# Gate and up projection of 20 feed-forward tiles by a seven-product 2x2 block scheme

## The chip, the cores and the metric

The kernel runs on one core of one Trainium2 chip. The metric is device microseconds of one execution, as the median of three runs. The engines are TensorE (PE, with its weight loads shown as PEld), VectorE (DVE), ScalarE (ACT), GpSimd (POOL) and SyncE (SP, which here issues the loads of the weights).

## The reference, cut to what matters

One decoder layer for 512 prompt tokens and 64 sample tokens, 576 in all, model width 1024. After three attention branches and an output projection comes the feed-forward part, in fp32. Its width is 2816, which is 22 tiles of 128:

```python
h = layer_norm(ALPHA * x + mix @ w_o, ln1_w, ln1_b)
ff_gate, ff_up = split(h @ w_ffn_in, 2)            # (576 x 1024) @ (1024 x 5632)
y = layer_norm(ALPHA * h + (silu(ff_gate) * ff_up) @ w_ffn_out, ln2_w, ln2_b)
```

## The kernel before

Everything is held transposed: features on the partitions, tokens along the free axis, in two halves of 288 tokens (`TH`). To keep fp32 accuracy each operand is split in two fp32r parts, a high part (the value rounded) and a low part (the rest). A 128 x 128 weight tile then takes three matmuls of 288 columns: high weights by low x, low weights by high x, high by high (lines 706 to 708).

A weight unit is 8 such tiles, 1024 x 128 values, 512 KB. SP loads it into one of four raw buffers `w_raw` (line 1057), as soon as the unit that was four before it has been used. ACT copies it into one of three buffers `w_hi` (line 1249). DVE writes the low part `w_lo` over the raw buffer (line 623; for some early units POOL does that).

A feed-forward tile `j` has a gate unit (`fg`) and an up unit (`fu`), each with two halves of tokens. Each of these four outputs is summed in one of three PSUM banks over 8 x 3 = 24 matmuls, so a tile has 96. For `fg`, ACT copies the bank (line 1279) and takes a tanh, and DVE makes the silu times two from both (line 1545). For `fu`, DVE multiplies by the bank (line 1568) and at once splits the result into `hidden_hi` and `hidden_lo` (lines 1571, 1572). These two hold all 22 tiles, since the output projection (`y`, lines 736 to 738) reads all of them.

One list, made by `schedule()`, sets the order of all work. Each engine walks it and issues its own part in that order, with semaphores between the engines. `ffn_order(j)` says in which order the four outputs of a tile come; the end of LayerNorm 1 (`center`, `norm`; `x_hi` on ACT, `x_lo` on DVE line 1590) is laced into tiles 0 and 1. Behind the loop over the tiles come the output projection and LayerNorm 2.

POOL adds the eight tiles of a LayerNorm mean in three steps (line 1204), issues some loads, and makes decay terms of one attention branch earlier (line 1145). It has nothing to do in the feed-forward loop.

Of the kernel before, what the change touches and what calls it, by code (L numbers as in the profile page):

```python
# [96 lines left out]
def ffn_order(j):  # L97

    if j == 0:
        return [("fg", 0, 0), ("fu", 0, 0), ("fg", 1, 0), ("fg", 0, 1), ("fu", 0, 1), ("fg", 1, 1)]  # L100
# [4 lines left out]

def weight_units():
# [47 lines left out]
    for j in range(FT_):  # L154
# [21 lines left out]
def schedule():  # L176
# [194 lines left out]
def build_decoder_layer(nc, a, outs_):  # L371
    ctx = ExitStack()
    with ctx:
# [189 lines left out]
        def moving(key, k):  # L563
# [55 lines left out]
        def split_lo(eng, u):  # L619
# [47 lines left out]
        def _(pe):  # L667
# [11 lines left out]
            def main(key):  # L679
# [5 lines left out]
                bank = take(main_bank(key))  # L685
# [1248 lines left out]
```

## Time and profile before

| what | value |
|---|---|
| median of three runs (lowest to highest) | 1152.78 us (1147.83 to 1152.86) |
| span of the profiled execution | 1145.7 us (no other time of it is given) |
| PE busy | 1090.5 us, 95%, 8128 matmuls |
| DVE, ACT, POOL busy | 641.9, 399.0, 210.3 us |
| matmuls of the gate/up and input projections | lines 706 to 708, 1504 each at x |
| moved by DMA | 105.82 MB |

Busy time is the sum of an engine's instructions. Matmuls overlap in PE's pipeline, so the pace of matmuls is read from the distance of two equal places in the loop, not from the duration of one. The feed-forward tiles run from about 693 us to about 978 us of the span.

### The profile page before, as it was taken

Reading aid. Unit: us, or ns where it says so; the run is one execution under the profiler, and the core shown is the slowest. Engines: PE = TensorE matmul, PEld = TensorE weight load, DVE = VectorE, ACT = ScalarE, POOL = GpSimd, SP = SyncE. Lnnn points to the kernel's source line nnn. Section 1 sums busy time; section 2 is a strip of 40 time slices with the busy share of each in tenths; the row PEclk is TensorE's granted clock in tenths of the full one; section 3 lists DMA queues with packets and bytes.
Section 4 is the critical chain, followed back from the end, with each engine's and each line's share of the span. In section 5 each row is a group of like instructions: output and inputs, shape, how many; then the busy total and the mean of one; then the engine's idle time right before and its main releaser. Section 6 shows DMA issues by size and latency. Waiting matters only on the chain.

```text
span 1145.7 us, 19556 instructions
## 1 busy us (share of the span) xinstructions
PE 1090.5 (95%) x8128; PEld 1051.9 (92%) x8128; DVE 641.9 (56%) x1022; ACT 399.0 (35%) x769; POOL 210.3 (18%) x266
## 2 busy tenths in 40 slices
PE   6799999998989998899999998999999999999996
PEld 5799888987989998889999987999999999999985
DVE  4833276345669989864654787444444444322455
ACT  3634255542345454315222255212221222111245
POOL 3521000012176563551000140000000000011130
PEclk9899899999999999999999999999999999999998
DMA  8456111135321111243232440332323232223422
GB/s 270 93 145 210 38 56 53 41 111 169 90 74 38 56 56 47 75 129 88 80 87 80 143 133 22 92 92 77 90 77 90 76 90 79 80 83 88 134 83 83
DMA packets 166582, 105.82 MB, mean 92 GB/s; under 512 B 11976, under 2 KB 161152, under 8 KB 166480
## 3 DMA queue, kind: packets, MB, share of 16 engines
q1 hardware_dynamic: 160944, 85.01, 25.8%
q0 software_dynamic: 4896, 17.21, 4.7%
q10 hardware_dynamic: 656, 2.36, 0.6%
q8 instruction: 65, 1.06, 0.4%
q14 instruction: 21, 0.17, 0.1%
HBM read 98.60 MB, written 6.95 MB: 92 GB/s over the span
## 4 chain that ended last, share of the span: by engine, by line
PE 79%; DVE 10%; ACT 3%; issue 3%; POOL 2%; DMA 2%; SPq 0%; DVEq 0%; ACTq 0%; POOLq 0%
PE bank L706 20%; PE bank L708 19%; PE bank L707 19%; PE bank L736 3%; PE bank L737 3%; PE bank L738 3%; PE bank L899 2%; DMA w_raw<-in_w_mem_kv 1%; DVE decay_q L1680 1%; PE bank L882 1%; DVE w_lo L623 1%; DVE a_masked L1693 1%; ACT probs L1297 1%; PE bank L1034 1%; POOL decay L1145 1%
## 5 line engine op out<-in xcount | busy, mean ns | idle before, releaser
L706 PE MATMUL bank<-x_lo,w_hi 128*128 128x288 f32 x1504 | 455.8, 303 | 3.4 <-DVE x_lo L1590 2.7
L708 PE MATMUL bank<-x_hi,w_hi 128*128 128x288 f32 x1504 | 445.0, 296 | 0.0
L707 PE MATMUL bank<-x_hi,w_lo 128*128 128x288 f32 x1504 | 444.8, 296 | 0.0
L706 PEld LDWEIGHTS bank<-x_lo,w_hi 128*128 128x128 f32 x1504 | 284.8, 189 | 11.9 <-issue 6.7
L707 PEld LDWEIGHTS bank<-x_hi,w_lo 128*128 128x128 f32 x1504 | 284.6, 189 | 0.2
L708 PEld LDWEIGHTS bank<-x_hi,w_hi 128*128 128x128 f32 x1504 | 284.0, 189 | 0.0
L1249 ACT ACTIVATE w_hi<-w_raw 128x1024 fp32r<-128x1024 f32 x158 | 164.3, 1043 | 268.9 <-PE bank L708 140.4
L623 DVE TENSOR_TENSOR w_lo<-w_raw,w_hi 128x1024 fp32r<-128x1024 f32 (+1 forms) x136 | 169.3, 1247 | 152.9 <-ACT w_hi L1249 152.4
L1279 ACT ACTIVATE gate<-bank 128x288 f32<-128x288 f32 x92 | 37.7, 410 | 190.0 <-PE bank L708 190.0
L1204 POOL TENSOR_TENSOR exp<-pre_norm 128x288 f32<-128x288 f32 x4 | 4.9, 1229 | 433.3 <-DVE pre_norm L1583 433.3
L737 PE MATMUL bank<-hidden_hi,w_lo 128*128 128x288 f32 x264 | 78.1, 296 | 0.0
L736 PE MATMUL bank<-hidden_lo,w_hi 128*128 128x288 f32 x264 | 78.1, 296 | 0.0
L738 PE MATMUL bank<-hidden_hi,w_hi 128*128 128x288 f32 x264 | 77.6, 294 | 0.0
L623 POOL TENSOR_TENSOR w_lo<-w_raw,w_hi 128x1024 fp32r<-128x1024 f32 x22 | 57.7, 2623 | 85.8 <-ACT w_hi L1249 85.7
L1545 DVE SCALAR_TENSOR_TENSOR gate<-gate,bank 128x288 f32<-128x288 f32 x44 | 20.0, 453 | 79.7 <-ACT gate L1279 79.7
L706 PE MATMUL bank<-branch_lo,w_hi 128*128 128x288 f32 x192 | 59.3, 309 | 0.0
L1145 POOL TENSOR_TENSOR decay<-hb 128x128 f32<-128x128 f32 (+1 forms) x124 | 51.8, 452 | 38.1 <-DVE decay_q L1680 31.4
L707 PE MATMUL bank<-branch_hi,w_lo 128*128 128x288 f32 x192 | 56.7, 295 | 0.0
L708 PE MATMUL bank<-branch_hi,w_hi 128*128 128x288 f32 x192 | 56.4, 294 | 0.0
L738 PEld LDWEIGHTS bank<-hidden_hi,w_hi 128*128 128x128 f32 x264 | 49.7, 188 | 0.0
L737 PEld LDWEIGHTS bank<-hidden_hi,w_lo 128*128 128x128 f32 x264 | 49.6, 188 | 0.0
L1568 DVE SCALAR_TENSOR_TENSOR gate<-gate,bank 128x288 f32<-128x288 f32 x44 | 20.0, 453 | 52.8 <-PE bank L708 52.8
(263 smaller groups left out, 1742.3 us busy)
## 6 DMA issues: line engine op xcount, KB each, us to landing
w_raw<-in_w_in SPq DMA_DIRECT2D x46, 512.0 KB, 3.9
w_raw<-in_w_ffn_in SPq DMA_DIRECT2D x44, 512.0 KB, 3.8
w_raw<-in_w_ffn_out SPq DMA_DIRECT2D x20, 512.0 KB, 3.7
w_raw<-in_w_o SPq DMA_DIRECT2D x14, 512.0 KB, 3.7
w_raw<-in_w_mem_kv SPq DMA_DIRECT2D x8, 512.0 KB, 5.1
mem_ring<-in_mem_k_s POOLq DMA_DIRECT2D x8, 512.0 KB, 6.0
mem_ring<-in_mem_v_s POOLq DMA_DIRECT2D x8, 512.0 KB, 4.0
w_raw<-in_w_ffn_out SPq DMA_DIRECT2D x10, 384.0 KB, 3.3
```

Source lines behind the costliest of these rows:

```text
L623: eng.tensor_tensor(WL[u % NRAW][:, 0:n, :], RAW[u % NRAW][:, 0:n, :], f32(WH[u % NHI][:, 0:n, :]), ALU.subtract).then_inc(w_lo_pool if u ...
L706: pe.matmul(bank[:, 0:n], wh, lo, start=(i == 0), stop=False)
L707: pe.matmul(bank[:, 0:n], wl, hi, start=False, stop=False)
L708: mm = pe.matmul(bank[:, 0:n], wh, hi, start=False, stop=(i == len(parts) - 1))
L736: pe.matmul(bank[:, 0:TH], wh, lo, start=(i == 0), stop=False)
L737: pe.matmul(bank[:, 0:TH], wl, hi, start=False, stop=False)
L738: mm = pe.matmul(bank[:, 0:TH], wh, hi, start=False, stop=(i == len(parts) - 1))
L899: mm = pe.matmul(bank[0:w, P * (i % 4):P * (i % 4) + w], k, q, start=True, stop=True)
L1145: pool.tensor_tensor(level_view(e[:, i, 0:w], m), v, v[:, :, m - 1:m].to_broadcast([P, w // (2 * m), 2 * m]), ALU.subtract)
L1249: return act.activation(dst, src, ACT.Copy)
L1279: act.activation(sig_dst(key), bank, ACT.Tanh, scale=0.5)\
L1545: dve.scalar_tensor_tensor(out=dst, in0=dst, scalar=1.0, in1=bank, op0=ALU.add, op1=ALU.mult)\
```

## The change

Tiles 0 and 1 stay as they are. For each tile from 2 to 21 (`pair` q = 0 to 19 in the new code: its gate and its up unit together) the weights are seen as a 2 x 2 block matrix, rows gate and up, columns the low four and the high four of the eight k tiles. The tokens are the other matrix, the k halves by the two halves of tokens. The product of two such 2 x 2 matrices is formed by seven block products and sums in place of eight block products. Each block product is 4 x 3 = 12 matmuls of 288 columns.

* **Weights.** SP loads the up unit into `up_weights` (A1, three buffers) and then the gate unit into `gate_weights` (A0, two buffers). POOL makes four sums or differences of 512 elements per partition: S1 = both halves of A1 added, S2 = S1 less the first half of A0, S4 = second half of A0 less S2, S3 = first half of A0 less first half of A1 (in place, in A1). ACT copies the high parts (`pair_hi`) of A0, S1, S2 with S4, and A1; DVE makes the low parts in place.
* **Tokens.** Four sums of x (`x_sum`), with high and low parts, are made once by DVE (`x_sums`; ACT copies the high parts), between tile 0 and tile 1 of the list.
* **Products.** In PE's order: P5(q), P7(q-1), P1(q), P4(q-1), P2(q), P3(q), P6(q). Even pairs use banks 0 to 2, odd pairs 3 to 5. The bank of P1 is copied by ACT (`snap s1`, into a gate buffer), then P6 adds to it and it is copied again (`s2`), then P7 adds to it and DVE adds the copy of P5 (`s5`, in a buffer `exp`) to give C22, the up value of half 1; then P4 adds to it, and what stands in it is the up value of half 0. C11 and C12, the gate values of both halves, are sums of a copy and a bank, on DVE.
* **Hidden tiles** are kept as one fp32 tile (`hidden`) and split into the two parts later: tiles 2 to 7 during the stage, the other 16 about and behind its end. The output projection's weights get raw and high buffers of their own. The LayerNorm 2 buffers move. In the residual sum x_lo is added first, then x_hi.

On ACT, in the steady feed-forward loop of the kernel before, an output's copy (`gate<-bank`) and a weight copy (`w_hi<-w_raw`) alternate in twos:

```order
L1279 ACTIVATE gate_79<-bank 128x288 [waits hidden_done,bank_free1,out_ready]
L1279 ACTIVATE gate_80<-bank 128x288 [waits hidden_done,bank_free2,out_ready]
L1249 ACTIVATE w_hi_59<-w_raw_52 128x1024 [waits out_ready,raw_in1]
L1249 ACTIVATE w_hi_60<-w_raw_53 128x1024 [waits out_ready,raw_in2]
L1279 ACTIVATE gate_77<-bank 128x288 [waits hidden_done,bank_free2,out_ready]
```

A weight copy waits for the load of a unit whose buffer was free one tile earlier. On ACT after, in the stretch of one pair in the middle of the stage (`gate_79<-gate_77` and `gate_80<-gate_78` are the tanh of half 0 and 1, `gate_78<-bank` is snap s2, `gate_77<-bank` snap s1, `exp<-bank` snap s5):

```order
L1642 ACTIVATE gate_79<-gate_77 128x288 [waits hidden_ready,summed_c11]
L1442 ACTIVATE pair_hi_161<-gate_weights_163 128x1024 [waits product,gate_in0]
L1442 ACTIVATE gate_78<-bank 128x288 [waits pair_gate,product]
L1642 ACTIVATE gate_80<-gate_78 128x288 [waits hidden_ready,summed_c12]
L1442 ACTIVATE pair_hi_161<-weight_sums_168 128x512 [waits product,combined]
L1442 ACTIVATE exp_76<-bank 128x288 [waits summed_c22,product]
L1442 ACTIVATE pair_hi_161<-weight_sums_168 128x1024 [waits product,combined]
L1442 ACTIVATE gate_77<-bank 128x288 [waits pair_gate,product]
L1442 ACTIVATE pair_hi_161<-up_weights_166 128x1024 [waits product,combined]
```

The copy of the gate weights, which waits for their load (`gate_in0`), now stands one row ahead of the copy of a bank to which the next product adds.

On DVE before, in the steady loop (one tile):

```order
L623 TENSOR_TENSOR w_lo_55<-w_raw_51,w_hi_61 128x1024 [waits w_hi]
L1545 SCALAR_TENSOR_TENSOR gate_79<-gate_79,bank 128x288 [waits silu_tanh]
L1545 SCALAR_TENSOR_TENSOR gate_80<-gate_80,bank 128x288 [waits silu_tanh]
L623 TENSOR_TENSOR w_lo_56<-w_raw_52,w_hi_59 128x1024 [waits w_hi]
L1568 SCALAR_TENSOR_TENSOR gate_79<-gate_79,bank 128x288 [waits bank_free1,out_ready]
```

No row there waits for POOL. On DVE after, the stretch of one pair from C12 on (`gate_78<-gate_78,bank`; the row of C22 is `hidden_192<-exp_75,bank`):

```order
L1914 TENSOR_TENSOR gate_78<-gate_78,bank 128x288 [waits snapped,product]
L1917 ISA [waits bank_free1]
L2140 SCALAR_TENSOR_TENSOR gate_80<-gate_80,gate_78 128x288 [waits pair_tanh]
L1898 TENSOR_TENSOR weight_sums_lo_175<-weight_sums_168,pair_hi_161 128x512 [waits combined,pair_hi]
L1921 TENSOR_TENSOR hidden_192<-exp_75,bank 128x288 [waits snapped,product]
L2148 SCALAR_TENSOR_TENSOR hidden_192<-gate_80,hidden_192 128x288 [waits summed_c22,pair_gate]
L1898 TENSOR_TENSOR gate_weights_lo_170<-gate_weights_163,pair_hi_161 128x1024 [waits combined,pair_hi]
```

The low part of S1 of the pair after next, which waits for a POOL sum (`combined`) and for ACT, stands between C12 and C22.

At the start of the stage, on DVE after, behind the gate of tile 1 in half 1 (`gate_80<-gate_80,bank`; `lower_tmp` holds a difference of biases, `hidden_189` is tile 1):

```order
L1816 SCALAR_TENSOR_TENSOR gate_80<-gate_80,bank 128x288 [waits silu_tanh]
L1859 TENSOR_TENSOR lower_tmp<-vectors 128x4 [waits ln_scaled]
L1860 TENSOR_TENSOR x_sum<-pre_norm 128x1152
L1864 SCALAR_TENSOR_TENSOR x_sum<-pre_norm,vectors,x_sum 128x288 [waits x_sum] x4
L1869 SCALAR_TENSOR_TENSOR x_sum<-pre_norm,lower_tmp 128x288 [waits bias_step] x4
L1882 TENSOR_TENSOR x_sum_lo<-x_sum,x_sum_hi 128x1152 [waits x_sum,x_sum_hi]
L1874 SCALAR_TENSOR_TENSOR x_sum<-pre_norm,vectors,x_sum 128x288 [waits x_sum] x4
L1882 TENSOR_TENSOR x_sum_lo<-x_sum,x_sum_hi 128x1152 [waits x_sum,x_sum_hi] x3
L1839 SCALAR_TENSOR_TENSOR hidden_189<-gate_79,bank 128x288 [waits bank_free0,out_ready]
L1839 SCALAR_TENSOR_TENSOR hidden_189<-gate_80,bank 128x288 [waits bank_free0,out_ready]
L1898 TENSOR_TENSOR weight_sums_lo_175<-weight_sums_168,pair_hi_161 128x512 [waits combined,pair_hi]
```

All token sums now stand ahead of the last two rows of tile 1 and of the first low part of the new weights; before, the row behind that gate was a weight's low part, and then those of tile 1.

The diff, cut to its core. The list (times in units of one product; pair q starts at 7q):

```diff
+PRODUCT_AT = {"P5": 0, "P1": 2, "P2": 4, "P3": 5, "P6": 6, "P7": 8, "P4": 10}
+BESIDE_AT = [
+    (1.1, "snap", "s5"), (3.1, "snap", "s1"), (5.1, "sum", "C11"), (5.5, "pair_tanh", 0), (5.9, "pair_gate", 0),
+    (7.05, "snap", "s2"), (7.3, "sum", "C12"), (7.6, "pair_tanh", 1), (8.0, "pair_gate", 1),
...
+    (-7.0, "pair_hi", "A0"), (-6.2, "pair_hi", "S1"), (-4.0, "pair_hi", "S24"), (-3.0, "pair_hi", "A1"),
...
-    for j in range(1, FT_):
-        for key in ffn_order(j):
-            out(key)
+    steps += [("x_sums", i) for i in range(4)]
+    for key in ffn_order(1):
+        out(key)
+    steps += pair_steps()
```

PE's new function, which `pair_steps` calls by name and pair:

```diff
+            def pair_product(name, q):
+
+                odd = 3 * (q % 2)
...
+                elif name == "P6":
+                    pe.wait_ge(snapped, SNAP_NO["s1", q])
+                    bank = BANK[odd]
+                elif name == "P7":
+                    pe.wait_ge(snapped, SNAP_NO["s2", q])
+                    bank = BANK[odd]
+                else:
+                    pe.wait_ge(summed_c22, q + 1)
+                    bank = BANK[odd]
+                pe.wait_ge(pair_lo, LO_NO[group, q])
+                for k in range(KH):
+                    wh, wl = PH[q % 2][:, hi_slot, k, :], lo[:, k, :]
+                    pe.matmul(bank[:, 0:TH], wh, xl[:, k, :], start=(first and k == 0), stop=False,
+                              skip_group_check=True)
+                    pe.matmul(bank[:, 0:TH], wl, xh[:, k, :], start=False, stop=False, skip_group_check=True)
+                    mm = pe.matmul(bank[:, 0:TH], wh, xh[:, k, :], start=False, stop=(k == KH - 1),
+                                   skip_group_check=True)
+                mm.then_inc(product, 1)
```

SP's loads, POOL's sums and DVE's sum C22:

```diff
+            for q in range(PAIRS):
+                c0 = (FIRST_PAIR + q) * P
+                if q >= 3:
+                    product_done(sp, "P4", q - 3)
+                sp.dma_start(A1[q % 3][:], w_ffn[:, :, FF + c0:FF + c0 + P]).then_inc(up_in[q % 3], 16)
+                if q >= 2:
+                    product_done(sp, "P2", q - 2)
+                sp.dma_start(A0[q % 2][:], w_ffn[:, :, c0:c0 + P]).then_inc(gate_in[q % 2], 16)
...
+                    if name == "S1":
+                        pool.wait_ge(up_in[q % 3], 16 * (q // 3 + 1))
...
+                        out, x, y, op = s1, up[:, 0:KH, :], up[:, KH:KT, :], ALU.add
+                    elif name == "S2":
+                        pool.wait_ge(gate_in[q % 2], 16 * (q // 2 + 1))
...
+                        out, x, y, op = s2, s1, gate[:, 0:KH, :], ALU.subtract
+                    elif name == "S4":
+                        pool.wait_ge(combined, COMBINE_NO["S2", q])
+                        out, x, y, op = s4, gate[:, KH:KT, :], s2, ALU.subtract
+                    else:
+                        out, x, y, op = up[:, 0:KH, :], gate[:, 0:KH, :], up[:, 0:KH, :], ALU.subtract
+                    pool.tensor_tensor(out, x, y, op).then_inc(combined, 1)
...
+                    product_done(dve, "P7", q)
+                    dve.wait_ge(snapped, SNAP_NO["s5", q])
+                    dve.tensor_tensor(HID[FIRST_PAIR + q][:, cols], EX[q % 2][:], BANK[odd][:, 0:TH], ALU.add)\
+                        .then_inc(summed_c22, 1)
```

## Rows read from the trace of the kernel before

**Rows 1.** The page's busy times: us, share of the span, instructions.

```profile
PE 1090.5 (95%) x8128; PEld 1051.9 (92%) x8128; DVE 641.9 (56%) x1022; ACT 399.0 (35%) x769; POOL 210.3 (18%) x266
```

**Rows 2.** Windows: length; busy us of PE, PEld, DVE, ACT, POOL; clock; DMA.

```profile
850.00:900.00 50.00, 50.00 (x379) 50.00 (x379) 22.51 (x40) 11.34 (x16) 0.00 (x0) 1.00 0.29 85
690.00:695.00 5.00, 3.48 (x13) 3.12 (x14) 4.90 (x10) 1.40 (x5) 1.38 (x1) 0.71 0.02 3
705.00:710.00 5.00, 3.45 (x16) 2.32 (x17) 5.00 (x13) 3.38 (x8) 0.00 (x0) 1.00 0.00 0
```

**Rows 3.** Timeline, DVE, feed-forward loop: start, us, what [idle before, releaser].

```profile
731.91 1.22 DVE L623 TENSOR_TENSOR w_lo<-w_raw,w_hi 128x1024 fp32r<-128x1024 f32 x1 [0.49 <-ACT w_hi L1249]
...
973.59 1.23 DVE L623 TENSOR_TENSOR w_lo<-w_raw,w_hi 128x1024 fp32r<-128x1024 f32 x1 [0.49 <-ACT w_hi L1249]
```

**Rows 4.** Timeline, PE and DVE, end of the feed-forward loop.

```profile
978.36 0.30 PE L736 MATMUL bank<-hidden_lo,w_hi 128*128 128x288 f32 x1
...
978.56 0.45 DVE L1568 SCALAR_TENSOR_TENSOR gate<-gate,bank 128x288 f32<-128x288 f32 x1 [1.91 <-PE bank L708]
```

**Rows 5.** Timeline, SP's issues (SPq), ACT and DVE, feed-forward loop.

```profile
711.39 0.37 SPq L1057 DMA_DIRECT2D w_raw<-in_w_ffn_in  x1
...
714.59 0.37 SPq L1057 DMA_DIRECT2D w_raw<-in_w_ffn_in  x1
...
715.12 1.06 ACT L1249 ACTIVATE w_hi<-w_raw 128x1024 fp32r<-128x1024 f32 x1 [2.36 <-DMA w_raw<-in_w_ffn_in]
...
718.74 1.06 ACT L1249 ACTIVATE w_hi<-w_raw 128x1024 fp32r<-128x1024 f32 x1 [0.53 <-DMA w_raw<-in_w_ffn_in]
...
803.64 0.41 ACT L1279 ACTIVATE gate<-bank 128x288 f32<-128x288 f32 x1 [2.03 <-PE bank L708]
...
804.08 0.45 DVE L1545 SCALAR_TENSOR_TENSOR gate<-gate,bank 128x288 f32<-128x288 f32 x1 [1.17 <-ACT gate L1279]
```

**Rows 6.** Timeline, POOL, a LayerNorm sum and an early low part.

```profile
644.40 0.80 POOL L1204 TENSOR_TENSOR exp<-exp,pre_norm 128x288 f32<-128x288 f32 x1 [2.39 <-DVE pre_norm L1583]
...
395.62 2.40 POOL L623 TENSOR_TENSOR w_lo<-w_raw,w_hi 128x1024 fp32r<-128x1024 f32 x1 [2.73 <-ACT w_hi L1249]
```

**Rows 7.** Timeline, DVE, the low parts of x in LayerNorm 1.

```profile
687.37 1.36 DVE L1590 SCALAR_TENSOR_TENSOR x_lo<-pre_norm,vectors,x_hi 128x288 fp32r<-128x288 f32 x3
```

**Rows 8.** Timeline, POOL and DVE, two stretches in the attention part.

```profile
331.64 4.46 POOL L1145 TENSOR_TENSOR decay<-hb 128x128 f32<-128x128 f32 x7
331.92 1.22 DVE L1675 TENSOR_TENSOR decay_k<-decay,hk 128x1024 f32<-128x1024 f32 x1 [5.39 <-ACT decay L1364]
...
333.06 0.49 DVE L1679 TENSOR_TENSOR q_exp_b<-exp_b,hq 128x128 f32<-128x128 f32 x1
...
347.48 0.28 DVE L1679 TENSOR_TENSOR q_exp_b<-exp_b,hq 128x128 f32<-128x128 f32 x1
...
356.38 2.44 POOL L623 TENSOR_TENSOR w_lo<-w_raw,w_hi 128x1024 fp32r<-128x1024 f32 x1 [4.62 <-ACT w_hi L1249]
...
356.49 3.27 DVE L1680 TENSOR_TENSOR decay_q<-decay,hq 128x896 f32<-128x896 f32 x1
...
365.19 1.08 DVE L1680 TENSOR_TENSOR decay_q<-decay,hq 128x896 f32<-128x896 f32 x1
```

**Rows 9.** Timeline, POOL and DVE, LayerNorm 1's end and tiles 0 and 1.

```profile
689.67 1.71 POOL L1204 TENSOR_TENSOR exp<-exp,pre_norm 128x288 f32<-128x288 f32 x1 [7.69 <-DVE pre_norm L1583]
...
691.62 1.21 DVE L623 TENSOR_TENSOR w_lo<-w_raw,w_hi 128x1024 fp32r<-128x1024 f32 x1
...
718.25 0.46 DVE L1545 SCALAR_TENSOR_TENSOR gate<-gate,bank 128x288 f32<-128x288 f32 x1 [0.81 <-ACT gate L1279]
...
724.16 0.45 DVE L1568 SCALAR_TENSOR_TENSOR gate<-gate,bank 128x288 f32<-128x288 f32 x1 [1.90 <-PE bank L708]
```

**Rows 10.** PE after that sum, timeline and then the chain of waits.

```profile
691.52 0.73 PE L1021 MATMUL bank<-exp,ones 128*128 128x288 f32 x2 [2.07 <-POOL exp L1204]
...
693.22 0.24 PE bank L706
```

More of the change, by code:

```diff
@@ L153, in weight_units @@
         plan([("o", c, half)])
-    for j in range(FT_):
+    for j in range(FIRST_PAIR):
         for kind, c0 in (("fg", j * P), ("fu", FF + j * P)):
@@ new lines, in build_decoder_layer @@
+        WL2 = [sb(f"w_lo_out{i}", [P, 8, P], F32R, even0 + 4096 * i) for i in range(NRAW)]
+        WH2 = [sb(f"w_hi_out{i}", [P, 8, P], F32R, even0 + 16384 + 4096 * i) for i in range(NHI)]
+        tile = T * 4
+        hid_at = [last0 + tile * i for i in range(3)] + [odd0 + 24576] + [raw0 + tile * i for i in range(12)] + \
+            [squares0 + tile * i for i in range(4)] + [y0, y0 + tile]
+        assert len(hid_at) == FT_ and odd0 + 24576 + tile <= y0 and tile * 12 <= 4096 * (NRAW + NHI)
@@ new lines, in build_decoder_layer @@
+        HID = [sb(f"hidden{j}", [P, T], F32, o) for j, o in enumerate(hid_at)]
+        GL = [sb(f"hidden_lo{j}", [P, T], F32R, o) for j, o in enumerate(hid_at)]
+        hi_at = {j: y0 + tile * (2 + i) for i, j in enumerate(EARLY_HI)}
+        sums0 = [proj0 + half * KT * T * 4 + 2 * tile * t for t in range(4) for half in range(2)]
+        hi_at |= {j: sums0[i // 2] + tile * (i % 2) for i, j in enumerate(LATE_HI)}
+        GH = [sb(f"hidden_hi{j}", [P, T], F32R, hi_at[j]) for j in range(FT_)]
@@ L550, in main_bank, with raw_of, lo_of_unit, hi_of_unit @@
             return OUT_NO[key] % MAIN_BANKS
+        bank_use = {}
         def out_saved(eng, key):
-            eng.wait_ge(bank_free[main_bank(key)], OUT_NO[key] // MAIN_BANKS + 1)
-        bank_use = {}
+            bank, count = bank_use[("out",) + key]
+            eng.wait_ge(bank_free[bank], count)
+        def raw_of(u):
+            return RAW[u % NRAW] if u < UNIT2 else RAW2[(u - UNIT2) % NRAW]
+        def lo_of_unit(u):
+            return WL[u % NRAW] if u < UNIT2 else WL2[(u - UNIT2) % NRAW]
+        def hi_of_unit(u):
+            return WH[u % NHI] if u < UNIT2 else WH2[(u - UNIT2) % NHI]
+        def product_done(eng, name, q):
+            eng.wait_ge(product, PRODUCT_NO[name, q])
         def saved(eng, *what):
@@ L684, in main @@
                     return
-                bank = take(main_bank(key))
+                bank = take(main_bank(key), "out", *key)
                 if kind == "mem":
@@ L721, in main_pair @@
                 keys = ("y", c, 0), ("y", c, 1)
-                banks = [take(main_bank(key)) for key in keys]
+                banks = [take(main_bank(key), "out", *key) for key in keys]
                 parts = OUTS[keys[0]]
@@ L728, in main_pair @@
                         bank = banks[half]
-                        if c == 0:
-                            pe.wait_ge(hidden_done, 2 * max(k for u, _, k in parts if u == unit) + half + 1)
                         for i, (u, tile, k) in enumerate(parts):
@@ L1008, in _ @@
                     (hgrn_out if rest[0] == "h" else values)(rest)
+                elif what == "product":
+                    pair_product(*rest)
                 elif what == "rms_sum":
@@ L1022, in _ @@
                     pe.wait_ge(y_ready, Y_NO[ln, half, c])
-                    pe.matmul(bank[:, 0:TH], ONES[:], Y[:, c, half * TH:half * TH + TH], start=False, stop=True)\
+                    pe.matmul(bank[:, 0:TH], ONES[:], Y[ln][:, c, half * TH:half * TH + TH], start=False,
+                              stop=True)\
                         .then_inc(mean_ready, 1)
@@ L1029, in _ @@
                         pe.wait_ge(folded, ln)
-                        mm = pe.matmul(bank[:, 0:TH], ONES[:], SQR[:, 0, :], start=True, stop=True)
+                        mm = pe.matmul(bank[:, 0:TH], ONES[:], SQR[ln][:, 0, :], start=True, stop=True)
                     else:
```

340 lines of the change are left out of this document (297 added, 43 removed), and 2 rows, old and new, of the table BESIDE_AT.

## The prediction

> **What bounds the kernel now.** I read the page's first part, then the windows, then the timeline of one feed-forward tile. TensorE (PE) is busy 95% of the span [rows 1], and in the gate/up stretch 50.00 of 50 us at a granted clock of 1.00, with VectorE (DVE) busy 22.5 us, ScalarE (ACT) 11.3 us and GpSimd (POOL) not at all [rows 2]. So the stage runs at the pace of its matmuls, and every other engine there has room. Its pace comes from two instructions of the same place in the loop, 19 tiles apart: (973.59 - 731.91) / 19 = 12.72 us a tile [rows 3], and 12.72 / 96 = 0.1325 us a matmul of 288 columns.
>
> **What is removed.** A pair by seven products has 7 x 12 = 84 matmuls of the same shape, against 96. 20 tiles x 12 x 0.1325 = 31.8 us less work for PE. A product takes 12 x 0.1325 = 1.59 us, a pair 11.13 us. This is the whole gain, and it holds only while PE never waits.
>
> **What is added beside PE.** Per pair, durations by size: DVE with two inputs in SBUF costs 0.43 us for 288 elements (three in 1.36 us: (1.36 - 0.50) / 2) and 1.14 us for 1024 (331.92 to 333.06) [rows 7, 8], by a straight line 0.65 for 512 and 1.26 for 1152. POOL shows 0.80 us for 288 and 2.40 for 1024 [rows 6]; 512 lies between, 1.29 by the line, and I take 1.25. DVE: 0.65 + 3 x 1.14 (low parts) + 3 x 0.43 + 4 x 0.45 = 7.2 us. ACT: 3 x 1.05 + 0.6 + 5 x 0.41 = 5.8 us. POOL: 4 x 1.25 = 5.0 us. Each is below 11.13 us, so by busy time all of it is hidden under PE. What counts is order and latency, and two places fail.
>
> **First wait, on ACT, before product P7.** The new order of PE after P2(q) is P3(q), P6(q), P5(q+1), P7(q). The gate weights A0 have two buffers, and P2(q) is the last reader of the one that pair q+2 needs; SP issues that load when P2(q) is done. On ACT the copy of those weights stands immediately ahead of the copy of P6's bank (`gate_78<-bank`), and P7(q) may add to that bank only after that copy. So P7(q) hangs on a load issued three products earlier. Count from the moment PE leaves P2(q): a consumer starts 0.20 us after the next matmul (978.36, 978.56) [rows 4]; issue to the copy's start is 715.12 - 711.39 = 3.73 us; the copy takes 1.05 [rows 5]; the bank copy takes 0.41, and the successor starts 0.03 us after (804.08) [rows 5], for PE I take 0.05. Sum 0.20 + 3.73 + 1.05 + 0.41 + 0.05 = 5.44 us, against 3 x 1.59 = 4.77 us of products: PE waits 0.67 us. The up weights' load A1 is issued one product before, on the same queue. The nearest row for a load behind another is 718.74 - 714.59 = 4.15 us, issued 3.20 us after one [rows 5], so 0 to 0.42 us more; full queueing would be 3.73 - 1.59 = 2.14 us more. I take 0.08: 0.75 us. It is paid by pairs 0 to 17, whose q+2 exists: 18 x 0.75 = 13.5 us (12 to 19.6).
>
> The Trainium skill, "DMA: Bandwidth & Descriptors", section "Anatomy of one DMA", has a fixed part of about 2.0 us in a transfer that is mostly the wait for the write's receipt, and bytes over 436 GB/s beside it; an estimate by that page is 3.2 us for 512 KB, and P7 would wait only 0.14 us, 2.5 us in all. The trace has 3.73 us here, so its rule of the size falls short; that a fixed part can overlap the load ahead speaks for the small end of the queueing.
>
> **Second wait, on DVE, before P4.** P4(q) reuses P7's bank and waits until DVE has added it into C22. In DVE's order there stand ahead of that sum: the sum C12, the gate of half 1, and the low part of S1 for pair q+2, which needs POOL's S2. POOL and DVE exclude one another when DVE reads two SBUF tensors: the 896-element product takes 1.08 us alone and 3.27 us when POOL has begun a 2.44 us subtraction 0.11 us before [rows 8]. When both queue, they take turns: inside a run of seven small POOL instructions the 128-element product takes 0.49 instead of 0.28 us, and that run 4.46 us [rows 8]. From the landing of A0 (time 0): ACT copies until 1.05 and 1.46; DVE's C12 until 1.94; ACT's tanh until 2.40; the gate instruction is ready at 2.43. POOL: S2 0.05 to 1.30, S4 1.40 to 2.65, then S3. Gate 2.65 to 3.08, S3 3.08 to 4.33, low part of S1 4.33 to 4.98, C22 until 5.43, P4 at 5.48. If S3 goes before the gate, the end is the same. PE comes to P4 after P7 and P1: 1.51 + 3.18 = 4.69. It waits 0.79 us, 18 x 0.79 = 14.2 us. Bounds: 0 if DVE's two run back to back ahead of S3; 18 us if each of the two POOL instructions takes 0.1 us more.
>
> The Trainium skill, "SBUF — State Buffer", section "Who interferes with whom", says that the instruction issued first holds the shared pair to its end. The gate is issued ahead of S3, and S3 ahead of S1's low part, so by that rule too S3 stands between them; a rule of pure priority for DVE would make this term 0, which is the first rival.
>
> **Start of the stage.** The token sums stand on DVE behind the gate of tile 1 (718.25, 0.45 us [rows 9]): 0.16 + 5 x 1.26 + 12 x 0.43 = 11.6 us until 730.3, then the two tile-1 products 0.95 us, then S1's low part 0.65 us: 731.9. PE leaves tile 1 about 724.0 (0.20 before 724.16 [rows 9]). So PE stands 7.9 us. POOL's sums for pairs 0 and 1 start when its last mean sum ends at 691.4 and delay the low part of 691.62 [rows 9], on which the mean's subtraction waits: about 1.0 us. After a gap of some 2 us (2.07) the matmul pace is 0.24 us and the window's clock 0.71 [rows 2, 10]; at the low level 14 matmuls lose 0.107 us each, 1.5 us. Together 10.4 us (8 to 14).
>
> **End of the stage.** P7(19) and P4(19) follow their own predecessors directly: 0.20 + 0.41 + 0.05 and 0.20 + 0.45 + 0.05, 1.4 us. The 14 late tiles cost DVE some 14 x 0.71 = 9.9 us behind the last product, but the output projection first reads 8 tiles that are ready (48 x 0.1325 = 6.4 us), and by then DVE has done 8 more: nothing, up to 2 us if the order of copies slips. Swapping the high and low x in the residual moves nothing.
>
> **Sum.** -31.8 + 13.5 + 14.2 + 10.4 + 1.4 = +7.7 us on the profiled execution's span of 1145.7 us, 1153.4 us. The page states no time of that execution beyond its span; the median of the runs is 1152.8 us, 7.1 us above it, and I carry these over: 1160.5 us, 0.7% slower. What can be told from no change is 0.5%, 5.8 us.
>
> **Rivals.** (1) DVE goes ahead of S3, and P4 does not wait: 1160.5 - 14.2 = 1146.3 us, faster. For it: DVE's low part is ready at 3.08, when the gate ends, with no gap in between. Against: the runs in which the two take turns [rows 8]. It decides at POOL's S3: begun before 3.1 us after the landing, P4 waits. If the loads are also quick, 1137. (2) The gaps pull the clock down: two gaps a pair, each followed by 10 matmuls at 0.24 us, lose 2 x 18 x 10 x 0.107 = 38.5 us: 1199 us. Against it, the window with PE busy 3.45 of 5 us has a clock of 1.00 [rows 2], and these gaps are shorter. The Trainium skill, "TensorE: Matmul & The Clock Gate", section "Why this matters for your kernels", warns of idle gaps in mid-kernel; only the gap at the start is like the one of the 0.71 row. (3) The two loads queue in full: 2.14 x 18 = 38.5 us, 1199 us; against it, 4.15 us above.
>
> **How the numbers follow.** Forecast 0.54, its own range 1151 to 1174 (the lower ends: -31.8 + 12 + 10 + 8 + 0.7; the upper: -31.8 + 19.6 + 18 + 14 + 3.4, less 2 because they hardly meet). Rival 1: 0.30, rivals 2 and 3: 0.08 each. Range 1137 to 1174: it leaves out the two dear rivals and little else. Slower by over 0.5% (above 1158.5): 0.65 of the forecast, 0.35, and 0.16, together 0.51. Faster (below 1147.0): three quarters of rival 1, 0.23. The rest, 0.26, within 0.5%.
>
> **What would show it.** In the profile after: gate/up matmuls 84 a pair; PE gaps of 0.7 us ahead of P7's first matmul, released by ACT's bank copy, whose engine waited for a `gate_weights` load; gaps of 0.8 us ahead of P4, released by DVE's C22, with POOL running just before; a pair of 12.6 us; one gap of 8 us at the first product, released by DVE. Wrong if pairs take 11.2 us, if P4's gap is missing (rival 1), if the clock in the pairs is under 0.95 (rival 2), or if the load takes over 5 us (rival 3).

## The result, and the profile after

The changed kernel takes 1176.24 us (median of four runs, 1174.32 to 1177.82), against 1150.46 us for the kernel before, of four runs too (the three given above with that kernel are among them): ratio 1.0222, 95% interval 1.0195 to 1.0249. It is slower, as forecast, but by about 26 us in place of 8, and outside the range. The span of the profiled execution is 1172.2 us, 26.5 above the one before.

The page's busy times of the changed kernel (columns as in [rows 1]), and two groups of its list of DMA issues (count, size of one, median us from issue to landing):

```profile
PE 1069.4 (91%) x7888; PEld 1021.7 (87%) x7888; DVE 715.5 (61%) x1074; ACT 469.9 (40%) x895; POOL 318.3 (27%) x346
```

```profile
up_weights<-in_w_ffn_in SPq DMA_DIRECT2D x20, 512.0 KB, 3.9
gate_weights<-in_w_ffn_in SPq DMA_DIRECT2D x20, 512.0 KB, 5.0
```

PE has 240 matmuls less and a longer span: its share went from 95% to 91%. The two loads of a pair have the same size, and the one that is issued second needs 1.1 us more.

What PE waited for in the whole span (line, releaser: us in total, times, longest):

```profile
PE bank L886 <- ACT gate L1442: 32.2, 18, 3.2
```

```profile
PE bank L886 <- DVE weight_sums_lo L1898: 7.9, 1, 7.9
PE bank L886 <- DVE hidden L1921: 5.0, 17, 0.5
```

These are the three predicted places: P7 behind ACT's bank copy s2, the first product behind DVE's first low part, P4 behind DVE's C22. Two of the counts take in a gap at the end of the stage, and the first pair's two gaps stand under another releaser; by the distances between matmuls there are 18 gaps before P7, as predicted, and 17 of 18 before P4. The sizes are another matter.

One pair in the middle of the stage, timeline of PE, SP, ACT, POOL and DVE (start, us, what, idle before and its releaser):

```profile
838.62 0.40 PE L886 MATMUL bank<-x_sum_lo,pair_hi 128*128 128x288 f32 x1 [1.71 <-ACT gate L1442]
...
844.24 0.37 SPq L1216 DMA_DIRECT2D up_weights<-in_w_ffn_in  x1
845.50 0.29 PE L889 MATMUL bank<-x_hi,pair_hi 128*128 128x288 f32 x1
...
845.82 0.37 SPq L1219 DMA_DIRECT2D gate_weights<-in_w_ffn_in  x1
850.29 0.29 PE L889 MATMUL bank<-x_sum_hi,pair_hi 128*128 128x288 f32 x1
...
850.81 1.06 ACT L1442 ACTIVATE pair_hi<-gate_weights 128x1024 fp32r<-128x1024 f32 x1 [3.17 <-DMA gate_weights<-in_w_ffn_in]
851.78 0.39 ACT L1442 ACTIVATE gate<-bank 128x288 f32<-128x288 f32 x1
852.21 1.29 POOL L1411 TENSOR_TENSOR weight_sums<-gate_weights,weight_sums 128x512 f32<-128x512 f32 x1
852.22 0.40 PE L886 MATMUL bank<-x_sum_lo,pair_hi 128*128 128x288 f32 x1 [1.64 <-ACT gate L1442]
...
853.29 0.52 DVE L2140 SCALAR_TENSOR_TENSOR gate<-gate,gate 128x288 f32<-128x288 f32 x1 [0.57 <-ACT gate L1642]
853.46 1.52 POOL L1411 TENSOR_TENSOR up_weights<-gate_weights,up_weights 128x512 f32<-128x512 f32 x1
853.82 1.71 DVE L1898 TENSOR_TENSOR weight_sums_lo<-weight_sums,pair_hi 128x512 fp32r<-128x512 f32 x1
855.45 0.44 DVE L1921 TENSOR_TENSOR hidden<-exp,bank 128x288 f32<-128x288 f32 x1
855.94 0.40 PE L886 MATMUL bank<-x_sum_lo,pair_hi 128*128 128x288 f32 x1 [0.28 <-DVE hidden L1921]
```

From one P7 to the next are 852.22 - 838.62 = 13.60 us, where a tile took 12.72 before [rows 3] and 84 matmuls take 11.13. The last matmul of P2 starts at 845.50, and SP issues the gate load at 845.82. ACT's copy of those weights starts 4.99 us after the issue, where the kernel before needed 3.73 [rows 5]. The bank copy behind it ends at 852.17, P7 starts at 852.22. From P7's first matmul back to the one before it are 1.93 us, 1.80 more than the pace. Then S4 (852.21) and S3 (853.46) on POOL: the gate instruction gets in between them, the low part of S1 waits out S3 (1.71 us in place of 0.65), and C22 follows it: P4 starts 0.57 us after the last matmul of P1, 0.44 more than the pace.

Windows of the changed kernel (columns as in [rows 2]): the start of the stage, then a stretch of pairs, and a piece of it.

```profile
730.00:735.00 5.00, 4.03 (x17) 4.06 (x18) 5.00 (x7) 2.29 (x5) 0.67 (x1) 0.50 0.00 0
850.00:900.00 50.00, 40.76 (x284) 39.13 (x283) 28.08 (x39) 20.44 (x34) 20.21 (x16) 0.97 0.22 64
870.00:875.00 5.00, 5.00 (x33) 5.00 (x33) 4.20 (x6) 1.56 (x3) 0.10 (x1) 0.81 0.00 0
```

The start itself, on DVE and PE, where [rows 9] has the place before:

```profile
725.59 3.90 DVE L1882 TENSOR_TENSOR x_sum_lo<-x_sum,x_sum_hi 128x1152 fp32r<-128x1152 f32 x3
...
730.13 0.69 DVE L1898 TENSOR_TENSOR weight_sums_lo<-weight_sums,pair_hi 128x512 fp32r<-128x512 f32 x1
...
730.97 0.58 PE L886 MATMUL bank<-x_sum_lo,pair_hi 128*128 128x288 f32 x1 [7.95 <-DVE weight_sums_lo L1898]
```

Against the full 50.00 us of the same stretch before [rows 2], PE is busy 40.76 us and no other engine is near its limit (DVE, the next, 28.08): the stage went from bound by matmuls to bound by latency. At the start PE stands until the token sums and the first low part are done, and then runs at a granted clock of 0.50, which is 1.2 GHz. Behind the longest gap before P7 (3.19 us, ahead of 867.37) the clock falls again, to 0.81 in the last row; behind the others, of 0.6 to 2.6 us, it stays at 1.00.

### The profile page after: what moved, and what is told of

Read it like the earlier page. It is cut to its first block, busy times and chain, and to the rows that moved or that the text cites. A ratio compares the mean times of both kernels' runs of the same rounds, so it can differ in the third digit from the quotient of the medians.

```text
span 1172.2 us, 19747 instructions
## 1 busy us (share of the span) xinstructions
PE 1069.4 (91%) x7888; PEld 1021.7 (87%) x7888; DVE 715.5 (61%) x1074; ACT 469.9 (40%) x895; POOL 318.3 (27%) x346
## 4 chain that ended last, share of the span: by engine, by line
PE 63%; DVE 13%; DMA 9%; issue 8%; ACT 6%; POOL 2%; SPq 0%; DVEq 0%; ACTq 0%; POOLq 0%
PE bank L811 12%; PE bank L812 11%; PE bank L813 11%; DMA gate_weights<-in_w_ffn_in 8%; PE bank L886 3%; PE bank L843 3%; PE bank L841 3%; PE bank L842 3%; PE bank L889 3%; PE bank L888 3%; PE bank L1048 2%; DMA w_raw<-in_w_mem_kv 1%; DVE decay_q L2018 1%; PE bank L1031 1%; ACT pair_hi L1442 1%
## 5 line engine op out<-in xcount | busy, mean ns | idle before, releaser
L811 PE MATMUL bank<-x_lo,w_hi 128*128 128x288 f32 x864 | 267.5, 310 | 4.9 <-DVE x_lo L1928 2.7
L812 PE MATMUL bank<-x_hi,w_lo 128*128 128x288 f32 x864 | 256.5, 297 | 0.0
L813 PE MATMUL bank<-x_hi,w_hi 128*128 128x288 f32 x864 | 256.3, 297 | 0.0
L811 PEld LDWEIGHTS bank<-x_lo,w_hi 128*128 128x128 f32 x864 | 164.8, 191 | 13.5 <-issue 8.4
L812 PEld LDWEIGHTS bank<-x_hi,w_lo 128*128 128x128 f32 x864 | 164.7, 191 | 0.2
L813 PEld LDWEIGHTS bank<-x_hi,w_hi 128*128 128x128 f32 x864 | 164.0, 190 | 0.0
L886 PE MATMUL bank<-x_sum_lo,pair_hi 128*128 128x288 f32 x320 | 99.0, 309 | 46.1 <-ACT gate L1442 32.2
L728 DVE TENSOR_TENSOR w_lo<-w_raw,w_hi 128x1024 fp32r<-128x1024 f32 x66 | 84.4, 1282 | 67.9 <-ACT w_hi L1442 67.6
L889 PE MATMUL bank<-x_sum_hi,pair_hi 128*128 128x288 f32 x320 | 95.1, 297 | 0.0
L843 PE MATMUL bank<-hidden_hi,w_hi_out 128*128 128x288 f32 x264 | 77.8, 295 | 0.0
```

The costliest lines, as they stand in the source:

```text
L728: eng.tensor_tensor(lo_of_unit(u)[:, 0:n, :], raw_of(u)[:, 0:n, :], f32(hi_of_unit(u)[:, 0:n, :]), ALU.subtract).then_inc(w_lo_pool if u i ...
L811: pe.matmul(bank[:, 0:n], wh, lo, start=(i == 0), stop=False)
L812: pe.matmul(bank[:, 0:n], wl, hi, start=False, stop=False)
L813: mm = pe.matmul(bank[:, 0:n], wh, hi, start=False, stop=(i == len(parts) - 1))
L843: mm = pe.matmul(bank[:, 0:TH], wh, hi, start=False, stop=(i == len(parts) - 1))
L886: pe.matmul(bank[:, 0:TH], wh, xl[:, k, :], start=(first and k == 0), stop=False, skip_group_check=True)
```

## The experiments

Eight kernels were run besides. Each time stands beside runs of the kernel before on the same chip. "Stage" is the time from the last matmul of tile 1 to the first of the output projection, where pure matmuls take 222.6 us. Rows 2 to 5 come from one chip, 6 to 8 from a second and the last from a third, so small differences between such groups are read from the ratios or the stage. Where a quoted expectation counts the experiments, it goes by the table: the A0 copy is the first, the load-dependent work the second, the up load the third.

| kernel | us | ratio to before (95%) | stage, us |
|---|---|---|---|
| changed | 1176.24 | 1.0222 (1.0195 to 1.0249) | 282.6 |
| A0 copy behind s2 | 1160.95 | 1.0096 (1.0060 to 1.0133) | 269.5 |
| load-dependent work behind the chain | 1131.66 | 0.9842 (0.9805 to 0.9878) | 236.0 |
| up load apart | 1156.95 | 1.0063 (1.0040 to 1.0086) | 261.7 |
| gate load first | 1205.97 | 1.0501 (1.0465 to 1.0537) | 312.1 |
| S3 behind C22 | 1171.86 | 1.0199 (1.0170 to 1.0228) | 273.5 |
| token sums spread | 1128.86 | 0.9831 (0.9803 to 0.9858) | 234.8 |
| sums spread, loads apart | 1130.32 | 0.9847 (0.9808 to 0.9886) | 234.4 |
| first pair's order too | 1123.78 | 0.9794 (0.9758 to 0.9830) | 230.0 |

**Why the gate load takes 5.0 us: up load apart.** A fourth buffer for the up weights lets the up load go out after P7: in one pair 5.3 us ahead of a gate load (846.74 and 852.04), and the next 7.4 us behind it (859.43).

```diff
-                 "a1": (even0 + 24576, even0 + 28672, even0 + 32768)}
+                 "a1": (even0 + 24576, even0 + 28672, even0 + 32768, squares0 + 2 * T * 4)}
+            def load_up(q):
...
+                if q >= 3:
+                    product_done(sp, "P7", q - 3)
...
+            for q in range(2, PAIRS):
+                load_gate(q)
...
+                    load_up(q + 1)
```

> The changed kernel with a fourth buffer for the up weights; the up load of pair q+3 is issued after P7(q), four to five us behind the gate load of pair q+2, in place of 1.6 us ahead of it. Orders on ScalarE, VectorE and GpSimd unchanged. Theory A (the gate load takes 5.0 us because the up load is just ahead of it on the same queue): gate load 3.8 us to landing, gap before P7 about 0.75 us in place of 1.8, gap before P4 as before or 0.1 to 0.4 us larger; 18 x 1.1 = 20 us less, about 1156 us. Theory B (the load is slow by itself in this stage, by its destination or by the other engines' traffic): landing stays at 5.0 us and the time within 3 us of 1176.

Its DMA issues, and what PE waited for:

```profile
up_weights<-in_w_ffn_in SPq DMA_DIRECT2D x20, 512.0 KB, 3.9
gate_weights<-in_w_ffn_in SPq DMA_DIRECT2D x20, 512.0 KB, 3.9
```

```profile
PE bank L888 <- ACT gate L1460: 12.3, 18, 1.7
...
PE bank L888 <- DVE hidden L1939: 5.4, 18, 0.5
```

The gate load fell to 3.9 us, the waits for s2 from 32.2 to 12.3 us, and the time to 1156.95 us, where 1156 was expected. Over the pace a gap before P7 has 0.74 us in the median; the prediction's chain gives 0.67 without queueing. The extra 1.1 us of the load was the other load just ahead of it. Its destination and the orders on ACT, DVE and POOL stayed as they were, so theory B falls. The changed kernel holds one such load itself: that of pair 2 goes out with no up load just ahead of it.

```profile
737.98 0.37 SPq L1219 DMA_DIRECT2D gate_weights<-in_w_ffn_in  x1
```

```profile
741.91 1.06 ACT L1442 ACTIVATE pair_hi<-gate_weights 128x1024 fp32r<-128x1024 f32 x1 [1.67 <-DMA gate_weights<-in_w_ffn_in]
```

Its copy starts 3.93 us after the issue, and the gap before P7(0), which hangs on it, has 0.78 us over the pace; the other seventeen have 1.64 to 3.36.

**The two loads swapped.**

```diff
+                if q >= 2:
+                    product_done(sp, "P2", q - 2)
+                sp.dma_start(A0[q % 2][:], w_ffn[:, :, c0:c0 + P]).then_inc(gate_in[q % 2], 16)
                 if q >= 3:
                     product_done(sp, "P4", q - 3)
                 sp.dma_start(A1[q % 3][:], w_ffn[:, :, FF + c0:FF + c0 + P]).then_inc(up_in[q % 3], 16)
-                if q >= 2:
-                    product_done(sp, "P2", q - 2)
-                sp.dma_start(A0[q % 2][:], w_ffn[:, :, c0:c0 + P]).then_inc(gate_in[q % 2], 16)
```

> The changed kernel with SyncE's two loads of a pair swapped: gate weights first, up weights 0.4 us behind. Theory A1 (loads of one queue are served in order of issue): gate load 3.8 to 4.0 us, up load about 5; the gap before P7 falls to 0.8 us, and GpSimd's S1, which waits for the up weights, pushes S2 and the low part of S1 back, so that the gap before P4 grows to about 1.5 us: about 1170 us. Theory A2 (both loads share the transfer engines in parallel): both land at about 5 us, the gap before P7 stays at 1.8 and that before P4 grows to 2 us or more: above 1195 us.

```profile
gate_weights<-in_w_ffn_in SPq DMA_DIRECT2D x20, 512.0 KB, 4.1
up_weights<-in_w_ffn_in SPq DMA_DIRECT2D x20, 512.0 KB, 5.4
```

The landings are those of A1: the first of two loads is hardly touched (4.1 us), the second pays. The Trainium skill, "DMA: Bandwidth & Descriptors", section "Two DMAs through the same engine are not ordered", says that within one queue of one engine descriptors start in order; these landings agree. The gap before P7, 0.9 us over the pace, is that of A1 too. The gap before P4 and the time, 1205.97 us, are what A2 named (2 us or more, above 1195 us): with the up load the later one, the waits for C22 grew to 37.5 us in 18 gaps, 2.1 each where A1 had 1.5, and the clock fell. So the swap shows which load pays; the price of the other load on POOL's side was too low in A1. Windows around one such gap, which ends at 862.09:

```profile
860.00:864.00 4.00, 2.05 (x13) 1.91 (x12) 3.90 (x4) 1.36 (x2) 2.82 (x2) 0.89 0.01 4
864.00:868.00 4.00, 4.00 (x24) 4.00 (x23) 3.45 (x5) 1.43 (x2) 0.00 (x0) 0.68 0.00 0
```

Matmuls start every 0.24 us there, some 15 of them (863.11 to 866.45). Over the stage, matmuls slower than the pace cost 21.2 us, against 7.4 in the changed kernel. So the low clock, the prediction's second rival, does occur in such a loop. The length of a gap alone does not say when: windows behind an idle time of 1.93 us (in the run with S3 behind C22) and behind one of 3.21 us (in the run with the A0 copy behind s2):

```profile
788.30:791.50 3.20, 3.13 (x13) 3.13 (x14) 1.65 (x3) 2.22 (x5) 1.28 (x1) 0.52 0.00 0
```

```profile
945.40:948.60 3.20, 3.16 (x24) 3.16 (x25) 3.09 (x4) 1.06 (x1) 0.00 (x0) 1.00 0.02 4
```

The shorter was followed by the low clock, the longer was not. What decides it stays open.

**The place of the A0 copy on ACT.**

```diff
-    (-7.0, "pair_hi", "A0"), (-6.2, "pair_hi", "S1"), (-4.0, "pair_hi", "S24"), (-3.0, "pair_hi", "A1"),
+    (-6.9, "pair_hi", "A0"), (-6.2, "pair_hi", "S1"), (-4.0, "pair_hi", "S24"), (-3.0, "pair_hi", "A1"),
```

> One edit to the changed kernel: on ScalarE the copy of the gate weights A0(q+2) stands directly behind the bank copy s2(q) in place of directly ahead of it. Theory A (the wait before P7 is only this order): the gap before P7, 1.8 us in the changed kernel, goes in all 18 pairs; the tanh of half 1, and with it gate, low part of S1 and C22 on VectorE, now hang on the load. Counted from PE's leaving P2: load landed 5.3, copy to 6.36, tanh to 6.7, gate held by GpSimd's S4 to about 8.3, S3 before the low part of S1 to 9.6, C22 to 10.65, P4 at 10.7 against 7.95: the gap before P4 grows from 0.44 to about 2.7 us and the pair takes 13.9 us in place of 13.6. Time 1176 to 1186 us. Theory B (the gap before P7 is lost time that no other wait inherits): pair 11.7 us, time about 1141 us.

What PE waited for, and one pair on POOL and DVE:

```profile
PE bank L886 <- DVE hidden L1921: 30.7, 18, 3.2
```

```profile
860.22 1.57 POOL L1411 TENSOR_TENSOR weight_sums<-gate_weights,weight_sums 128x512 f32<-128x512 f32 x1
860.22 0.46 DVE L2140 SCALAR_TENSOR_TENSOR gate<-gate,gate 128x288 f32<-128x288 f32 x1 [3.38 <-ACT gate L1642]
860.74 1.61 DVE L1898 TENSOR_TENSOR weight_sums_lo<-weight_sums,pair_hi 128x512 fp32r<-128x512 f32 x1
862.27 0.44 DVE L1921 TENSOR_TENSOR hidden<-exp,bank 128x288 f32<-128x288 f32 x1
```

No wait for s2 is left, and the wait before P4 went from 5.0 to 30.7 us: the load is inherited, as theory A says, at 1.8 us a pair over the pace (33.1 / 18) and not 2.7. In the row shown the gate did not stand behind S4; it started with it and S4 was stretched to 1.57 us. The time, 1160.95 us, lies between the two forecasts, and A's mechanism is the one that the waits show.

**All that hangs on the load behind the chain.** The A0 copy goes behind the tanh as well, and S1's low part behind C22:

```diff
-    (-7.0, "pair_hi", "A0"), (-6.2, "pair_hi", "S1"), (-4.0, "pair_hi", "S24"), (-3.0, "pair_hi", "A1"),
-    (-5.6, "pair_lo", "S1"), (-4.1, "pair_lo", "A0"), (-3.2, "pair_lo", "S24"), (-2.1, "pair_lo", "A1"),
+    (-6.3, "pair_hi", "A0"), (-6.2, "pair_hi", "S1"), (-4.0, "pair_hi", "S24"), (-3.0, "pair_hi", "A1"),
+    (-4.5, "pair_lo", "S1"), (-4.1, "pair_lo", "A0"), (-3.2, "pair_lo", "S24"), (-2.1, "pair_lo", "A1"),
```

> Two edits to the changed kernel: on ScalarE the copy of A0(q+2) stands behind s2(q) and the tanh of half 1; on VectorE the low part of S1(q+2) stands behind C22(q). All that hangs on the load of the next weights but one then stands behind all that P7 and P4 of this pair wait for. Theory A (both gaps are order alone): gaps before P7 and P4 go, pair 11.13 to 11.3 us, 35 + 8 us of gaps and some 4 us of slow first matmuls are gone: about 1129 us, faster than the kernel before (1150). Theory B (TensorE waits for the weights themselves, or for the engines' work): the pair stays above 12.5 us, time above 1155 us, with a gap before P5 or P1 released by a low part.

```profile
800.00:850.00 50.00, 50.00 (x379) 50.00 (x378) 40.94 (x49) 25.69 (x43) 26.47 (x19) 1.00 0.30 85
```

PE is busy all 50 us, as before the change, and DVE 41 of 50, though the gate load still takes 5.0 us. Two places in a list were worth 44.6 us: 1131.66 us, 1.6% faster than the kernel before, and theory A's 1129 within 3 us. In the pairs one gap is left, 1.44 us over the pace before P7(10). This is the seven-product scheme as it was meant.

**POOL's S3 between the gate and the low part of S1.**

```diff
                     else:
+                        if q >= 2:
+                            pool.wait_ge(summed_c22, q - 1)
                         out, x, y, op = up[:, 0:KH, :], gate[:, 0:KH, :], up[:, 0:KH, :], ALU.subtract
```

> The changed kernel with one wait more, on GpSimd: S3(q+2) begins only when VectorE has made C22(q). All other orders as in the changed kernel, so the copy of A0 still stands ahead of s2. Theory A (the gap before P4 comes from S3, which runs between the gate and the low part of S1): the low part of S1 takes 0.6 us in place of 1.7, C22 ends 1.1 us earlier, the gap before P4, 0.44 us with 0.11 us of a slow first matmul, goes in all 18 pairs, and that before P7 stays at 1.8 to 2.0: about 10 us less, 1166 us. Theory B (S4, not S3, or the copies on ScalarE set the time of C22): the gap before P4 stays, 1174 to 1178 us.

```profile
856.10 0.69 DVE L1900 TENSOR_TENSOR weight_sums_lo<-weight_sums,pair_hi 128x512 fp32r<-128x512 f32 x1
856.71 0.45 DVE L1923 TENSOR_TENSOR hidden<-exp,bank 128x288 f32<-128x288 f32 x1
```

The low part of S1 takes 0.69 us in place of 1.71, and the wait before P4 is gone but for that of the last pair. The stage is 9.1 us shorter, as theory A says. The median is only 4.4 us shorter, by the ratios 2.6, and the span 1.6: in the profiled execution tile 0 began at 689.00 us, in the changed kernel at 683.06, and ahead of that both kernels are the same. Of these 5.9 us, 2.9 come in the first 60 us and 2.5 between 505 and 511 us, where the granted clock is 0.51; at the same place in the changed kernel (501 to 506) it is 1.00. Why the two executions differ there stays open.

**The start: token sums spread.** On the kernel with the load-dependent work behind the chain, DVE's steps are put where DVE is idle:

```diff
-    steps += [("x_sums", i) for i in range(4)]
...
+    early = [("x_sums", 0), ("x_sums", 1), ("x_lo", 0), ("pair_hi", "S1", 0), ("pair_hi", "A0", 0), ("x_sums", 2)]
...
+    out(first[4])
+    more = [("pair_lo", "S1", 0), ("pair_hi", "S24", 0)]
...
+    out(ffn_order(1)[0])
+    more = [("x_sums", 3), ("pair_hi", "A1", 0), ("pair_lo", "S24", 0)]
```

> The kernel with all load-dependent work behind the bank chain (second experiment), and the token sums and the first low parts spread on VectorE: the first three sums of x ahead of tile 0's last product, the other steps between tile 1's, each low part ahead of the product that needs it. The work is the same. Theory A (the 8.1 us at the first product are VectorE's queue, and VectorE is half idle in the 12 us ahead of it): the gap goes or falls under 1 us, and with it the stretch at clock 0.50 behind it, 2 us: 1120 to 1123 us against 1131.7. Theory B (the work only moves: banks of tiles 0 and 1 come free later and TensorE waits there): a gap of 3 us or more in tile 1 or in the first pair, 1127 to 1133 us.

```profile
735.91 2.28 DVE L1913 TENSOR_TENSOR weight_sums_lo<-weight_sums,pair_hi 128x1024 fp32r<-128x1024 f32 x1
738.12 2.28 DVE L1913 TENSOR_TENSOR up_weights_lo<-up_weights,pair_hi 128x1024 fp32r<-128x1024 f32 x1
740.32 0.44 DVE L1922 TENSOR_TENSOR gate<-gate,bank 128x288 f32<-128x288 f32 x1
...
741.69 0.58 PE L900 MATMUL bank<-x_sum_lo,pair_hi 128*128 128x288 f32 x1 [5.60 <-issue]
```

Theory B: the gap at the first product went from 8.1 to 0.8 us and 5.8 came back before P7 of pair 0, so the stage is only 1.2 us shorter (234.8 against 236.0). Two low parts of 1.22 us, stretched to 2.28 by POOL's sums, stand ahead of C11 (740.32), and s2 on ACT stands behind the tanh that needs C11. The next run moves these, and with them two bank copies on ACT.

**The first pair's order too.**

```diff
+            ("pair_lo", "A1", 0), ("sum", "C11", 0), ("x_lo", 2), ("pair_hi", "A0", 1), ("pair_tanh", 0, 0),
+            ("pair_lo", "A0", 1), ("pair_gate", 0, 0), ("x_lo", 3)]
+    late_lo = {("sum", "C22", 0): ("pair_lo", "S24", 1), ("pair_hidden", 1, 0): ("pair_lo", "A1", 1)}
```

> The kernel with the token sums spread, with one more edit in the first pair: on VectorE the low parts of S2/S4 and of the up weights of pair 1 stand behind C22(0) in place of ahead of C11(0), and on ScalarE s5(0) and s1(0) stand ahead of the copies for pair 1. Theory A (the gap of 5.8 us before P7(0) in the run before is C11(0) queued on VectorE behind two low parts that GpSimd's sums stretched to 2.28 us each, and s2(0) on ScalarE behind the tanh that needs C11): the gap falls below 1 us, the stretch at the low clock behind it goes, and the pair stage takes 226 to 228 us from P5(0) on: 1121 to 1124 us. Theory B (VectorE has more work in these 20 us than time): the gap turns up at another product of pairs 0 or 1, 4 us or more in sum, 1126 to 1130 us.

```profile
PE 1062.4 (95%) x7888; PEld 1021.4 (91%) x7888; DVE 735.1 (66%) x1074; ACT 468.1 (42%) x895; POOL 326.6 (29%) x346
```

1123.78 us, as theory A says: 2.1% faster than the kernel before, and PE back at 95%. The gap before P7(0) is 0.4 us and the low clock behind it is gone. Part of theory B holds too: gaps of 2.3 and 0.6 us turn up before P4(0) and P4(1), and from P5(0) on the stage takes 229.0 us, just over the 226 to 228 of theory A. This is the fastest version tried.

**Both at once: sums spread and loads apart.** The edits are those of two experiments above.

> The same kernel with the fourth buffer for the up weights and the up loads apart from the gate loads (third experiment). Theory A (in the second experiment's order the load's time is hidden, 11 us of a pair lie between its landing and its first reader): the time is that of the run beside it within 2 us, though the gate load falls from 5.0 to 3.9 us. Theory B (late loads still cost a gap now and then, as the single one of 1.45 us): 1.5 to 5 us less.

1130.32 us against 1128.86, with the gate load at 3.9 us: theory A. Once the load is off the chain its length is worth nothing that these runs can tell.

## Why the prediction was right and wrong

Both waits, their places, their releasers and nearly their counts were as predicted. The sign came out too, but it had been given a chance of 0.51 and hung on terms that were off by more than the forecast of +7.7 us. Here is the sum by its own terms, on the span. Measured is what the distances between starts of successive matmuls have over 0.1325 us.

| term | predicted, us | measured, us |
|---|---|---|
| matmuls removed | -31.8 | -31.8 (20 x 12.72 less 1680 x 0.1325) |
| wait before P7 | +13.5 (12 to 19.6) | +35.3 in 18 pairs |
| wait before P4 | +14.2 (0 to 18) | +7.5 in 17 pairs |
| PE stands at the start | +7.9 | +8.1 |
| POOL's sums ahead of the mean | +1.0 | 0.0 |
| matmuls slower than the pace | +1.5 | +7.4 |
| end of the stage | +1.4 | +1.4 |
| ahead of and behind the stage | 0 | -1.6 |
| sum | +7.7 | +26.3 (spans: 26.5) |

**The step that failed** is "I take 0.08: 0.75 us" for the gate load behind the up load. The load took 1.26 us more than the single one (4.99 against 3.73), not 0.08, and P7 waited 1.96 us a pair: 21.8 us over the term, more than the whole miss of 18.8 us on the span. The text had the row of 4.15 us, but of a load issued 3.20 us behind another [rows 5]; here the distance is 1.58 us. It also had full queueing at 2.14 us, put it aside as a rival with little chance, and left it out of the term's bounds. The runs show something between, 1.1 to 1.3 us; the load's median of 5.0 us stands at the very sign (over 5 us) that was set for that rival. A term that hangs on a distance that no row shows should have kept both ends. The experiments with the loads apart and with the loads swapped show the cause; without the queueing the prediction's chain of latencies fits, 0.74 us in the median against 0.67. The estimate of 3.2 us, 0.14 us of wait, went by another path: the fit in the Trainium skill, "DMA: Bandwidth & Descriptors", section "Anatomy of one DMA", is for transfers issued by GpSimd. These loads are issued by SyncE, and alone they took 3.7 to 3.9 us.

**The wait before P4** was smaller than predicted because C22 ended 5.10 us after the load's landing, where 5.43 was worked out (855.89 less 850.79, the landing in the chain of waits). On the same count one gap is 0.44 us and not 0.79. S3 began 2.67 us after the landing (853.46), on the side of 3.1 us that the prediction had named for a wait, and the mechanism stands: without S3 in between the wait is gone. The Trainium skill, "SBUF — State Buffer", section "Who interferes with whom", has a DVE instruction with two SBUF inputs contend with a GpSimd instruction that reads SBUF; the 1.71 and 0.69 us of the same instruction, with S3 and without, agree. The first rival fell with that: DVE did not go ahead of S3.

**Slow matmuls.** Of the 7.4 us, 4.0 are 38 first matmuls after a gap, each with 0.24 us to the next in place of 0.13. The prediction did not have them, though a wait that is short costs one of these every time. The other 3.4 us are 31 matmuls at the clock of 1.2 GHz, 17 at the start (14 predicted) and 14 behind the one gap of 3.2 us.

**POOL's sums** did delay the low part on DVE, to 2.29 us at 690.50, but tiles 0 and 1 took 39.8 us with them (683.06 to 722.86) and without (684.18 to 723.96; the tiles begin there and not at about 693 us). So something else there was as late; what, is not shown.

**From span to time.** The forecast carried 7.1 us over the span; the profiled execution took 1174.32 us, 2.1 above its span, and the median is 4.0 above it. Every later execution stands 1.8 to 3.0 us above its own span, so the one with the span of 1145.7 us was probably the 1147.83 us, the fastest of the three, and 7.1 us joined two different executions. That error has the other sign and hid 3 us of the miss.

## What to carry to other kernels

In a loop that is bound by one engine, a copy that waits for a transfer should stand behind everything in its engine's queue that the bound engine needs this round; then the transfer's length matters little (5.0 or 3.9 us made no difference that could be told once the order was right, and 19 us before). When two loads go out on one queue within 2 us, let the second pay for the first (here 1.1 to 1.3 us on 3.9), and keep full queueing in the range. Moving a wait off one engine is not enough if the next engine's chain hangs on the same load: the first reordering gave 15 us back, the second 29 more.

## What the runs showed of the hardware that was not expected

A pair of 512 KB loads on one queue, 1.58 us apart, landed after 3.9 and 5.0 us in the median; 0.41 us apart, after 4.1 and 5.4; 5.3 us apart, after 3.9 and 3.9.

In the loop of the changed kernel three gate loads took over 5.5 us: those issued at 859.4, 903.0 and 944.4, with 6.53, 5.63 and 5.94 us. Behind each of the three issues, by 2.1 to 3.3 us, began one 16 KB packet of a queue that the profile marks `instruction`; for 858 to 867 us the list of queues has it so (packets, MB, share):

```profile
q8 instruction: 1, 0.02, 0.6%
```

The same goes for the loads over 5.5 us in the runs with the A0 copy behind s2 (two) and with the load-dependent work behind the chain (three). That the packet is what slows the load is not tested. At the start, where five loads went out in 5.4 us, single ones took up to 8.6 us.

In the pairs of the changed kernel each of the 37 gaps with 0.28 us or more of idle time is followed by one matmul that takes 0.21 to 0.24 us to the next, though the granted clock behind all but one of them is 1.00. Idle times of 0.6 to 2.6 us before P7 and of 0.3 before P4 left the clock at 1.00 there; with the loads swapped, 0.7 to 1.2 and 2 us or more in each pair went with a clock of 0.83 in six of the sixteen windows of 10 us from 740 to 900 us.
